# Splitting one projection of a fused transformer kernel into three pieces, and moving a score product ahead of the chunk outputs

## The reference, cut to what matters

```python
h = rms_norm(x, norm_mix[l])
proj = h @ w_in[l]
qkv_a, z_a, b_a, a_a, q_b, kv_b, gate_b, u_c = split_columns(proj)
y_a = gdn_mixer(qkv_a, z_a, ...)   # gated delta rule, chunks; output rms_norm(o) * silu(z)
y_b = nsa_mixer(q_b, kv_b, ...)    # compressed, selected and windowed attention, summed with gates
y_c = pool_mixer(u_c, ...)
y = jnp.concatenate([y_a, y_b, y_c], axis=-1)
x = x + y @ w_out[l]
h = rms_norm(x, norm_ffn[l])
x = x + jnp.square(jax.nn.relu(h @ w_ffn1[l])) @ w_ffn2[l]
```

## Time and profile before

| | us |
|---|---|
| median of 3 runs | 1025.2 (1024.95 to 1025.54) |
| the profiled execution | 1027.41 |
| its span, first to last instruction | 1025.7 |
| PE busy in the span | 970.9 |
| DVE busy in the span | 435.5 |
| ACT busy in the span | 180.8 |
| mean granted TensorE clock | 0.984 of full speed |

### The profile page before, as it was taken

How to read it: one execution, slowest core, us unless ns; L and a number is a source line. 1 busy time by engine, 2 the same in 40 slices (tenths; PEclk the granted TensorE clock), 3 DMA queues, 4 the chain that set the end, 5 groups by cost and what they waited for, 6 DMA issues and landing times.

```text
span 1025.7 us, 15493 instructions
## 1 busy us (share of the span) xinstructions
PE 970.9 (95%) x6427; PEld 541.7 (53%) x6427; DVE 435.5 (42%) x811; ACT 180.8 (18%) x416; POOL 29.3 (3%) x92
## 2 busy tenths in 40 slices
PE   7999999999999999999999999999888998889996
PEld 6788866576666665568764533333222332223332
DVE  2868577174555566402223663722222122222213
ACT  2233433110000000204342101110001011001111
POOL 8100000000000000000000000000000000000000
PEclk9999998999999999999999999999999999999999
DMA  8424022584766689562243799999999999999994
GB/s 353 177 94 161 3 83 83 203 356 188 285 284 282 282 347 423 210 233 75 90 165 134 307 409 427 427 427 426 427 427 427 427 427 425 428 429 427 416 413 192
DMA packets 30097, 302.49 MB, mean 295 GB/s; under 512 B 5968, under 2 KB 6096, under 8 KB 11472
## 3 DMA queue, kind: packets, MB, share of 16 engines
q1 hardware_dynamic: 30032, 301.53, 71.8%
HBM read 300.47 MB, written 1.05 MB: 294 GB/s over the span
## 4 chain that ended last, share of the span: by engine, by line
PE 72%; DMA 17%; SPq 5%; DVE 2%; ACT 1%; issue 1%; POOL 0%; DVEq 0%; POOLq 0%
PE PS L1639 11%; PE PS L1250 10%; PE PS L1985 9%; PE PS L1245 9%; PE PS L1688 8%; DMA slot<-in_moe_w_up_dram 8%; PE PS L2004 6%; SPq L673 5%; DMA AR<-in_moe_w_up_dram 4%; DMA XH<-in_moe_w_up_dram 4%; PE PS L1961 3%; PE PS L1470 2%; PE PS L1586 2%; DMA slot<-in_moe_w_down_dram 2%; PE PS L1936 1%; PE PS L1682 1%
## 5 line engine op out<-in xcount | busy, mean ns | idle before, releaser
L1639 PE MATMUL PS<-XH,slot 128*128 128x256 f32 x512 | 113.3, 379 | 1.7 <-DVE XH L2513 0.9
L1639 PEld LDWEIGHTS PS<-XH,slot 128*128 128x128 f32 x512 | 97.1, 190 | 21.3 <-issue 8.9
L1245 PE MATMUL PS<-XH,slot 128*128 128x256 f32 x432 | 97.6, 383 | 0.0
L1245 PEld LDWEIGHTS PS<-XH,slot 128*128 128x128 f32 x432 | 80.7, 190 | 12.4 <-issue 1.2
L2004 PE MATMUL PS<-slot,ATT 128*32 128x512 f32 x576 | 67.0, 619 | 9.6 <-DMA slot<-in_moe_w_up_dram 9.6
L1985 PE MATMUL PS<-slot,ATT 128*32 128x512 f32 x544 | 65.3, 607 | 8.8 <-DMA slot<-in_moe_w_gate_dram 4.9
L1250 PE MATMUL PS<-slot,XH 128*128 128x256 f32 (+4 forms) x224 | 71.7, 476 | 0.0
L1985 PE MATMUL PS<-slot,MASKS 128*32 128x512 f32 x576 | 64.3, 594 | 1.8 <-DMA slot<-in_moe_w_down_dram 1.3
L2562 DVE SCALAR_TENSOR_TENSOR AR<-AR 128x384 f32<-128x384 f32 (+1 forms) x112 | 59.9, 612 | 0.0
L1961 PE MATMUL PS<-AR,DIAG 128*128 128x512 f32 x120 | 57.6, 605 | 0.0
L1250 PEld LDWEIGHTS PS<-slot,XH 128*128 128x128 f32 x224 | 42.0, 190 | 26.1 <-issue 14.8
(11 more groups left out here) (469 smaller groups left out, 1188.8 us busy)
## 6 DMA issues: line engine op xcount, KB each, us to landing
slot<-in_moe_w_up_dram SPq DMA_DIRECT2D x18, 2048.0 KB, 30.7
slot<-in_w_ffn_dram SPq DMA_DIRECT2D x16, 2048.0 KB, 8.3
slot<-in_moe_w_gate_dram SPq DMA_DIRECT2D x16, 2048.0 KB, 36.9
slot<-in_moe_w_down_dram SPq DMA_DIRECT2D x16, 2048.0 KB, 36.8
AR<-in_ada_w_dram SPq DMA_DIRECT2D x16, 1536.0 KB, 14.2
AR<-in_moe_w_gate_dram SPq DMA_DIRECT2D x9, 2048.0 KB, 34.1
AR<-in_moe_w_down_dram SPq DMA_DIRECT2D x8, 2048.0 KB, 36.2
AR<-in_moe_w_up_dram SPq DMA_DIRECT2D x8, 2048.0 KB, 34.5
```

Of the source, the lines that this page charges most:

```text
L1245: ins = pe.matmul(dst, w[:, c * width + col:c * width + col + n], HT[:, c, :], start=(c == 0), stop=(c == KC - 1))
L1639: ins = pe.matmul(PS[:, b, (f % 2) * T:(f % 2 + 1) * T], slots[s][:, c * 512 + f * P:c * 512 + (f + 1) * P], HT[:, c, :], start=(c == 0), ...
```

## The change

The projection `z1`, so far one run of 8 chunks, becomes three pieces of 4, 2 and 2 chunks with other products between them; it gets bank 7 for itself, and the six banks go round without it. The selected scores of tile 1 (`ss1`) move from behind the chunk outputs to before the third piece of `z1`. In the table, `z1` now stands behind `ss1`. `mixed(1, 0, 6, 7)`, which uses bank 7, moves from behind the scores to between `qs1` and `o1`. On DVE the masking of `ss1` moves ahead of the taking of `o0`; on ACT `take_z(1)` and the exponentials of `ss1` move ahead.

```diff
-    g += [("cmp", "D"), ("x0", "D"), ("pm0", "A"), ("pm1", "A"), ("S", "D"), ("z1", "A"), ("ks10", "D"), ("ks11", "D"), ("kct", "D")]
-    g += scores("w", 1) + [("py0", "D"), ("py1", "D"), ("x1", "D"), ("cs_low", "D"), ("cs_high", "D"), ("o0", "D"), ("qs10", "D"), ("qs11", "D")]
-    g += [("o1", "D")] + scores("s", 1) + turns("s", 0) + turns("w", 0) + turns("c", 0) + [("no0", "A")]
+    g += [("cmp", "D"), ("x0", "D"), ("pm0", "A"), ("pm1", "A"), ("S", "D"), ("ks10", "D"), ("ks11", "D"), ("kct", "D")]
+    g += scores("w", 1) + [("py0", "D"), ("py1", "D"), ("x1", "D"), ("cs_low", "D"), ("cs_high", "D")] + scores("s", 1)
+    g += [("z1", "A"), ("o0", "D"), ("qs10", "D"), ("qs11", "D"), ("o1", "D")] + turns("s", 0) + turns("w", 0) + turns("c", 0) + [("no0", "A")]
...
+            elif GROUPS[k][0] == "z1":
+                BANKS.append(7)
             elif k >= SIX_FROM:
-                BANKS.append((k - SIX_FROM) % 6)
+                BANKS.append((k - SIX_FROM - (k > order["z1"])) % 6)
...
-            take_z(1)
             nsa_exps(1, "w")
             compressed_exps(0)
             compressed_exps(1)
+            take_z(1)
+            nsa_exps(1, "s")
             act.wait_ge(sems["o_sumsq"], 1)
             rsqrt(OR, O2, 1.0 / HD, M2[:, 0:12], sems["o_rnorm"])
             nsa_probs(0, "s")
             nsa_probs(0, "w")
             nsa_compressed(0)
-            nsa_exps(1, "s")
...
-                if c0 == 0:
-                    pe_open(pe, f"z{i}")
                 return token_major(bank(f"z{i}")[:, 0:GW], weights("in2"), 512, P, GW, i, chunks=(c0, c1))
...
             ins.then_inc(filled, 1)
-            project_z(1, 0, KC).then_inc(filled, 1)
+            bank_free(pe, "z1")
+            project_z(1, 0, 4)
             wait_emptied(pe, "S")
             from_state("ks1", 3)
...
             nsa_scores(1, "w")
             pool_out()
+            project_z(1, 4, 6)
             pe.wait_ge(sems["rhs_ready"], 1)
             solve(1, lambda h: RHS[:, h, :])
             nsa_compressed_scores()
+            nsa_scores(1, "s")
+            project_z(1, 6, KC).then_inc(filled, 1)
...
             mixed(0, 0, 6, 7)
             within_tile(0)
             from_state("qs1", 0)
-            within_tile(1)
-            nsa_scores(1, "s")
             bank_free(pe, "out10")
             mixed(1, 0, 6, 7)
+            within_tile(1)
...
             nsa_compressed_masked(1)
+            nsa_masked(1, "s")
             b = wait_filled(dve, "o0")
...
             nsa_compressed_probs(0)
-            nsa_masked(1, "s")
             nsa_compressed_probs(1)
```

More of the change, by code:

```diff
@@ L1518, in _ @@
                     nsa_scores(0, "w")
+                    bank_free(pe, "z0")
                     project_z(0, 0, KC).then_inc(filled, 1)
```

## The result

| | before | after |
|---|---|---|
| median, four runs each, us | 1025.08 (1023.96 to 1025.54) | 1038.66 (1038.33 to 1040.54) |
| the profiled execution, us | 1027.41 | 1038.69 |
| its span, us | 1025.7 | 1037.0 |
| mean granted TensorE clock | 0.984 | 0.980 |

The change makes the kernel slower by 13.6 us; the ratio is 1.013, with an interval of 1.0114 to 1.0146. Between the two traces the difference is 11.3 us, 2.3 less, since the traced execution of before lies that far above its median and that of after does not.

A forecast was written before the change was run, and what follows sets the result against it. The prediction took PE to be what everything waits for, held before `mixed` by the `out0` transfer. Its shifts, 9.2 + 1.0 - 2.5 + 1.0 = +8.7 us on the 1025.2 median, gave 1033.9 us, range 1029.5 to 1039.5.

The forecast's parts named there:

- term 3: From `mixed` to the end of `o1`: one more `mixed` and some low clock after the long wait, +1.0 us.
- Terms 1 and 2: `z1` complete only at 152.7 us; `out0`, issued then, lands 7.6 us later and PE starts `mixed` 9.2 us later.
- rival (a): At the first `mixed`: the fill of `out0` does not hold PE, so the kernel is faster, 1022.3 us; chance 6%.
- rival (c): Between the pieces of `z1`: the clock falls already at PE's new 1.0 us wait near 143, 1037.9 us; chance 12%.
- Rival (b): After PE's waits: the clock comes back at once, so no low clock is paid, 1030.0 us; chance 12%.
- Term 4: From `o1` to the next use of `out0`: early scores shorten it despite a new 2.4 us wait for DVE, -2.5 us.
- Term 5: A second fall of the clock behind PE's waits of 2.4 and 0.9 us, +1.0 us, bounds 0 and 2.8.
- rival (d): After the stage: a later stage waits for a transfer issued without regard to PE, time stays 1025.2 us; chance 4%.

The follow-up runs named there:

- e1: Kernel before with the fill of `out0` put in slot 5 in place of slot 2, so issued early, at 97 us: 1026.78 us, ratio 1.0005.
- e3: Kernel before with only SP's fill of `out0` (still slot 2) held until the compressed scores are filled: 1033.07 us, ratio 1.0064.
- e5: Kernel after with eight needless products of 512 columns on PE inside the wait for `out0`: 1035.01 us, ratio 1.0105.
- e6: Kernel after with DVE norming the compressed weights before the chunk outputs and ACT emptying the turned weights before its sum-of-squares wait: 1031.72 us, ratio 1.0065.
- e4: Kernel after with `z1` whole again at its old place, early scores kept, `out0` in slot 2: 1025.51 us, ratio 0.9990.
- e9: Kernel before with `out0` in slot 5, its fill held until `x0` is filled: 1024.33 us, ratio 0.9994.
- e10: Kernel after, `z1` in three pieces, with `out0` in slot 5 held until `x0`, norming early on DVE, ACT's emptying first: 1021.26 us, ratio 0.9972.
- e8: Kernel after with `z1` whole at its old place, `out0` in slot 5 held until `x0`, norming early, ACT's emptying first: 1022.67 us, ratio 0.9969.
- e2: Kernel after with the fill of `out0` put in slot 5, not held: 1028.76 us, ratio 1.0022.
- e7: Kernel after with `out0` in slot 5, its fill held until `x0` is filled: 1025.77 us, ratio 1.0006.

## Why the prediction was right, and where its sum was off

The median after, 1038.66, lies in the range, on the side forecast, 4.8 us above the 1033.9. That the range holds it is partly luck: its upper end had 4.3 us for a low clock in term 3 that didn't come, and these cover the 3.1 outside the sum and the little by which terms 2 and 5 passed their bounds. By its terms, from the two traces:

| term | forecast | measured | from |
|---|---|---|---|
| 1, `z1` complete | 152.7 | 152.67 | 151.11 + 1.56 |
| 2, wait for `out0` | +9.2 | +9.5 | 160.73 against 151.19 |
| 3, `mixed` to the end of `o1` | +1.0 | +0.5 | 9.80 against 9.28 |
| 4, `o1` to the six of `mixed` | -2.5 | -2.5 | without the low clock |
| 5, second fall of the clock | +1.0 | +3.0 | see below |
| sum | +8.7 | +10.5 | 194.52 against 184.00 |

**Terms 1 and 2** hold to a few hundredths and to 0.3 us: the landing took 7.9 instead of 7.6. The reading that the transfer and not DVE held PE, against the name in the earlier trace rows, is shown by e1 and e3, and with it rival (a) falls. The wait of 0.90 near 143 (1.0 forecast) is there, but the clock stayed at 1.00 behind it, and rival (c) did not come. Its time, 1037.9, is nearest to the median all the same, by another cause. The small wait of 0.3 for `py1` was not there; other rows made up for it, so the hundredths are luck.

**Term 3.** The low clock cost `mixed` 1.7 (3.55 to the next start, against 1.82) and `o0` 0.7 (2.17 against 1.48), 2.4 together where 2.9 was taken; e5, with PE kept busy, has neither. Rival (b) fails by that.

**Term 4** came as worked out: 3.86 to the compressed turn (3.75), 1.65 to the values (1.71), 3.09 from there at full clock. The wait is 2.54 (2.4) and ACT's 0.82 (0.89). But the prediction had the start of the values hang on DVE's norming, with ACT's emptying behind it. ACT, by its wait for the sum of squares, is done only at 175.98, and by that row would have held them by itself; that the sum came out is luck in this part. e6, which moves both, shows that the two orders together made the wait.

**Term 5 is the term that was mis-sized,** 3.0 where 1.0 was taken. From the first values to the six of `mixed` it is 5.39 us against 3.09, and the six themselves and what follows up to the third use cost 0.69 more: 3.0, above even the bound of 2.8. That bound priced the six alone. The clock fell 5 us earlier, on the values (2.83 for 1.53) and the second compressed turn (1.46 for 0.83). A bound for a fall of the clock has to take in all the work behind the wait, not the next large item. In e6, with only the wait of 0.89 left, there is no fall.

**What lies outside the sum.** From the stage's end on, the traces differ by 0.8 more (0.3 ahead of the identity's products, 0.5 behind): 10.5 + 0.8 is the 11.3 between the spans. The shift does reach the end, so rival (d) didn't come. The last 2.3 are the traced execution of before against its median. The prediction saw that difference and applied the shift to the median as if it were the same in every execution. That seems to be wrong in a way that can be named, though it isn't shown: term 3 takes away the 10 us of low clock that stand in the trace of before, and e1, e4 and e9, with gaps of 0.85, 0.55 and 0.86, had 3.4, 3.3 and 0 us of it. In the runs beside e1 to e4, the nine executions of before above 1026 us had a mean clock of 0.980 to 0.983 and the sixteen below it 0.985 to 0.992; the traced one had 0.984. (Beside e9 and e10 the two groups overlap.) The traces point the same way: the span less the stage is 974.7 to 979.0 us in the twelve, and 976.0 in before, in their middle. So the excess of its execution doesn't show outside the stage. A typical execution of before then has, it seems, less low clock to lose, and the change costs more against it. Other executions of before were not traced, so the place stays open. The same offset is in the experiments: the totals of e8, e9 and e10 gain 2.3 to 3.8 us less than their stages.

## What to carry to other kernels

When a product is split or moved, look for the transfer that is issued on its completion: work that stood behind the issue and covered it stands ahead of it now, at the full price of the landing (here 8 us). A queue in program order deserves the same look: DVE idled for 11 us with the norming that PE needed next behind two takings, and ACT's emptying stood behind a wait of its own. Moving two calls on each was worth 5.8 us of the stage together. Both held PE at nearly the same time, which the row of one wait doesn't tell. When a version with one more edit is measured, set it against the old kernel with the same edit. Price a wait together with the low clock behind it, over all the work up to its return, and where the trace of before holds a low stretch after a short gap, don't take it as present in every run.

## What the runs showed of the hardware

- A 2 MB fill that lands beside runs of 64 by 64 products cost PE 1.23 and 2.33 us of "issue" (e1, e2). Held back behind them, and landing beside larger products from some 135 to 144 us, it left no such row (e7, e9).
- After gaps of 0.85 and 0.86 us at the same place the clock was low for 3.4 us once and not at all the other time (e1, e9); after gaps of 0.55 and 0.56 us, 3.3 us and not at all (e4, e8). After the long waits, with the same `mixed` and `o0` first behind them, it was back 5.2 us after PE resumed in the kernel after, and 13 us after in e3.
- Eight needless products in a wait kept the clock, and the kernel with them was 3.4 us shorter in the stage, 2.5 of it ahead of the second wait, and 3.6 in the median (e5).
- The landing of the same 2 MB took 7.6 (before, e8) to 8.2 us (e9) and once 8.5 (e10) when issued behind the small products, and 8.5 and 8.6 beside them (e1, e2).
